# Seven block products instead of eight in the first feed-forward matmul too

## The chip, the cores and the metric

One NeuronCore of one Trainium2 chip. The metric is the device time of one launch in microseconds (us), taken as the median of several runs; one further execution was recorded by the hardware profiler, and all rows below are of that execution.

## The reference

One decoder layer over 512 tokens of width 1024, all in float32: a mixer (a gated chunk MLP beside a state-space scan), a feed-forward layer and a gated per-layer embedding, with a final RMSNorm. The part that the change touches is

```python
hid = jax.nn.relu(rmsnorm(h, norm_mlp_g[i]) @ w_ff1[i])   # (512 x 1024) @ (1024 x 4096)
h = h + (hid * hid) @ w_ff2[i]                            # (512 x 4096) @ (4096 x 1024)
gate = jax.nn.sigmoid(rmsnorm(h, ple_norm_g[i]) @ w_ple_gate[i])
h = h + gate * (p[i] @ w_ple_proj[i])
```

## The kernel before

Every large product is computed from operands split in two: `hi` is the value rounded to float32r, `lo` is what is left. A product of two split operands takes three matmuls, hi by hi, hi by lo and lo by hi (`product`, L1485 to L1489). ScalarE writes a `hi` (a copy with rounding), VectorE then the `lo` (value minus `hi`). An operand tile has 128 partitions; one matmul uses a 128x128 stationary block and streams up to 512 columns into a PSUM bank. There are eight banks: `acc` has four and `side` has four.

The stages in order: the input projection with the mixers beside it (L1567 to L1662), the output projection, the PLE product (L1695 on), whose result ScalarE brings to `y` and SyncE stores to `ple_dram`, the feed-forward layer, the gate product and the output.

The feed-forward layer goes in four units `u` of 1024 hidden columns. Inside a unit there are forms: weight blocks of 512x512, each kept as hi and lo in a ring of three (`ring`). The first matrix gives four forms (`product_f1`, L1705): the whole normed x (in `b_hi`, `b_lo`, transposed, 512 tokens) streams against them, two forms add up in one PSUM bank, four banks per half unit; that is 4 forms x 4 blocks x 4 k-tiles x 3 matmuls of 512 columns. ScalarE applies relu and square bank by bank (`relu`, `square`, L668 to L685).

The second matrix is done in the Strassen-Winograd way: the hidden block (512 tokens x 1024) and the weight block (1024 x 1024) are cut in quarters, and seven products of a sum of quarters with a sum of quarters replace the eight of the plain way (`product_f2`, L1724; PRODUCTS and A_FORMS, L22 and L23). The sums of hidden quarters, S1 to S4, are made by VectorE (`s_add`, L1296). The sums of weight quarters, T1 to T4, are made by GpSimd's queue: DMAs that add one SBUF tile to another (`t_add`, L549), or, for T1, that add a quarter from HBM to a reloaded one (`reload_b12`, L440). Four buffers `quarter` hold the quarters. A form of the second matrix has 2 x 4 x 3 = 24 matmuls of 512 columns. Two of its seven products stay in `side` over all units; the other five go to `acc` and VectorE adds them to `h` (`h_add`, `h_finish`, L1337 to L1365).

Each engine's order is written out by hand: SyncE's loads from L448 on, ScalarE's list from L892 on, VectorE's from L1367 on, TensorE's from L1748 on. Engines meet in semaphores: `form_hi` and `form_lo` count split half-forms, `ff_step` products, `hid_hi` and `hid_lo` split hidden blocks, `h_added` results. A form is split in two halves of 128x1024 by ScalarE and VectorE (`split_form`, L650 and L1286) once the product three forms back has ended. After the last unit the transposes `turn_norm(2, ..)` of h (L1552) stand in the middle of the last product and of the gate products, and `split_gate` (L591 and L995) prepares the gate's weights.

Of the kernel before, what the change touches and what calls it, by code (L numbers as in the profile page):

```python
# [5 lines left out]
P = 128  # L6
F32 = mybir.dt.float32
# [11 lines left out]
TILES = (2, 3, 0, 1)  # L19
UNITS = 4  # L20
STEPS = 30
# [4 lines left out]
SUMS = ("T3", "T2", "T1", "T4")  # L26


def build_layer(nc, a, out):
# [26 lines left out]
    with ExitStack() as ctx:  # L56
# [8 lines left out]
        with ExitStack() as early:  # L65
# [6 lines left out]
            gain = sb("gain", [P, 2, D], where=early)  # L72

        def form(name, tiles, width):

            hi = sb(name + "_hi", [P, tiles, width], F32R)
            with ExitStack() as first:
                raw = sb(name + "_raw", [P, tiles, width], where=first)
            lo = sb(name + "_lo", [P, tiles, width], F32R)
            return hi, raw, lo  # L80

        quarter = [sb(f"quarter{i}", [P, 4, 512]) for i in range(2)]
        ring = {0: form("ring0", 4, 512)}
        ring[2] = form("ring2", 4, 512)
        ring[1] = form("ring1", 4, 512)
        quarter += [sb(f"quarter{i}", [P, 4, 512]) for i in range(2, 4)]
        a2 = form("a2", 4, 512)
        s_form = {n: form(f"s{n}", 4, 256) for n in (3, 4, 1, 2)}
        a1 = sb("a1", [P, 4, 512])
        tmp = sb("tmp", [P, 4, 512])  # L90
        with ExitStack() as early:
            conv = sb("conv", [P, 2, 512], where=early)
            xs_t = sb("xs_t", [P, 2, 512], where=early)
# [3 lines left out]
        a11_hi = sb("a11_hi", [P, 4, 256], F32R)  # L97
        a11_lo = sb("a11_lo", [P, 4, 256], F32R)
# [17 lines left out]
        b_hi = sb("b_hi", [P, KT, SEQ], F32R)  # L116
        b_lo = sb("b_lo", [P, KT, SEQ], F32R)
# [77 lines left out]
        f1_landed = [[sem(f"f1_landed{i}{p}") for p in range(2)] for i in range(3)]  # L195
        q_landed = [[sem(f"q_landed{i}{p}") for p in range(2)] for i in range(4)]
        ff_step = sem("ff_step")
        form_hi, form_lo = sem("form_hi"), sem("form_lo")
        gate_hi, gate_lo = sem("gate_hi"), sem("gate_lo")
        t_landed = [[sem(f"t_landed{i}{p}") for p in range(2)] for i in range(2)]  # L200
# [72 lines left out]
        plan += [(("xt", 2, j, q), (2 * j + q + 2) % 4) for j in range(NS) for q in range(2)]  # L273
# [25 lines left out]
        def form_end(n):  # L299

            u, j = divmod(n, FORMS)
            return STEPS * u + (4 * j + 4 if j < 4 else 16 + 2 * (j - 4) + 2)

        def f1_use(n):

            return sum(m % 3 == n % 3 and m % FORMS < 4 for m in range(n + 1))

        def product_end(u, name):

            return STEPS * u + 16 + 2 * PRODUCTS.index(name) + 2  # L310

        def form_count(u, name, p):

            return 2 * (FORMS * u + 4 + PRODUCTS.index(name)) + p + 1

        def hid_bank(u, i):

            return (i + (2 if u else 0)) % 4

        def sum_landed(eng, u, name, p):  # L320

            eng.wait_ge(t_landed[QUARTER[name]][p], 16 * (2 * u + (1 if name in ("T3", "T2") else 2)))

        ADDS = ("T3 right", "T3 above", "T2", "T4", "B21", "B22")
        LAST_ADDS = ("B11 above", "B11 right", "T1 right", "T1 left", "C21", "C12")
# [5 lines left out]
        LO_COUNT = {"A11": 1, "S3": 2, "S2": 3, "S1": 4, "A22": 6, "A12": 6, "S4": 7}  # L331
# [5 lines left out]
        def _(sp):  # L337
# [71 lines left out]
            def load_f1(n):  # L409

                u, e = divmod(n, FORMS)
                b, kh = 2 * u + e // 2, e % 2
                if n >= 3:
                    sp.wait_ge(ff_step, form_end(n - 3))
                else:
                    sp.wait_ge(acc_full, 4 * (OUT + 4) if n < 2 else 4 * (PLE + 1))
# [1396 lines left out]
```

## Time and profile before

| what | value |
|---|---|
| median of 3 runs | 748.6 us (747.29 to 748.61) |
| the profiled execution, its own time | 747.09 us |
| its span, first to last instruction | 745.3 us |
| TensorE busy | 735.0 us, 99% |
| VectorE busy | 454.1 us, 61% |
| ScalarE busy | 382.9 us, 51% |
| GpSimd busy | 107.3 us, 14% |

In the rows PE is TensorE's matmuls, PEld its weight loads, which overlap them, DVE VectorE, ACT ScalarE, POOL GpSimd and SP SyncE. A group of instructions is told by its line in the kernel and by the tiles that it writes and reads. A matmul's duration is its latency; successive matmuls overlap, so their pace is read from their starts. A `[1.38 <-DVE h L1022]` behind a row is idle time of the engine ahead of it and what ended it.

### The profile page before, as it was taken

To read this page: it belongs to the slowest core of one execution; us is meant where nothing else is said; L and a number is where in the kernel's file an instruction comes from. 1 tells how busy PE (TensorE), PEld (TensorE's weight loads), DVE (VectorE), ACT (ScalarE), POOL (GpSimd) and SP (SyncE) were. 2 spreads that over 40 slices of the span, in tenths; PEclk is the share of its full clock that TensorE was granted. 3 is DMA by queue.
4 is the path that set the end of the run, shared out by engine and by line. 5 is a ranking of instruction groups with operands and counts; after the bars stand their busy time and mean duration, and the time that the engine had idled before them with its cause. 6 is when DMAs were issued, how large, how long until landed. Compare 5 with 4: busy or idle time off the path is not lost.

```text
span 745.3 us, 8676 instructions
## 1 busy us (share of the span) xinstructions
PE 735.0 (99%) x3396; PEld 606.4 (81%) x3396; DVE 454.1 (61%) x500; ACT 382.9 (51%) x516; POOL 107.3 (14%) x88
## 2 busy tenths in 40 slices
PE   8999999999999999999999999999999999999996
PEld 7888877788878888888888888888888888888884
DVE  5556794576667465546444952576454942589764
ACT  6524456644674833304564633572266524575775
POOL 1031000766455000000012000020001000200000
PEclk9999999999999999999999999999999999999998
DMA  9732223342241163100976685477727792585311
GB/s 332 210 86 86 87 85 99 124 143 86 93 162 57 57 214 125 58 29 14 373 234 148 140 297 150 84 143 231 227 63 156 192 275 97 118 192 178 106 57 56
DMA packets 47872, 105.58 MB, mean 142 GB/s; under 512 B 4668, under 2 KB 6360, under 8 KB 47832
## 3 DMA queue, kind: packets, MB, share of 16 engines
q1 hardware_dynamic: 40968, 84.03, 33.7%
q0 software_dynamic: 5632, 16.78, 12.4%
q10 hardware_dynamic: 1232, 4.23, 1.6%
q8 instruction: 27, 0.44, 0.2%
q14 instruction: 13, 0.11, 0.0%
HBM read 88.21 MB, written 4.23 MB: 124 GB/s over the span
## 4 chain that ended last, share of the span: by engine, by line
PE 98%; DMA 1%; ACT 0%; issue 0%; DVE 0%; SPq 0%; DVEq 0%
PE acc L1487 28%; PE acc L1489 28%; PE acc L1488 28%; PE side L1549 3%; PE side L1488 2%; PE side L1489 2%; PE side L1487 2%; PE side L1646 2%; PE side L1613 1%; PE side L1653 1%; PE side L1641 1%; DMA gain<-in_norm_mix_g 1%; PE acc L1570 0%; PE side L1593 0%; PE side L1594 0%; PE side L1633 0%
## 5 line engine op out<-in xcount | busy, mean ns | idle before, releaser
L1487 PE MATMUL acc<-w_hi,a_hi 128*128 128x512 f32 x256 | 104.5, 408 | 0.0
L1489 PE MATMUL acc<-w_hi,a_lo 128*128 128x512 f32 x256 | 100.2, 391 | 0.0
L1488 PE MATMUL acc<-w_lo,a_hi 128*128 128x512 f32 x256 | 99.9, 390 | 0.0
L1487 PE MATMUL acc<-b_hi,ring_hi 128*128 128x512 f32 x256 | 99.7, 390 | 0.0
L1489 PE MATMUL acc<-b_hi,ring_lo 128*128 128x512 f32 x256 | 99.7, 389 | 0.0
L1488 PE MATMUL acc<-b_lo,ring_hi 128*128 128x512 f32 x256 | 99.7, 389 | 0.0
L664 ACT ACTIVATE ring_hi<-quarter 128x1024 fp32r<-128x1024 f32 x56 | 56.5, 1051 | 51.3 <-PE acc L1489 34.7
L1293 DVE TENSOR_TENSOR ring_lo<-ring_raw,ring_hi 128x1024 fp32r<-128x1024 f32 x32 | 38.6, 1223 | 67.0 <-ACT ring_hi L664 67.0
L1293 DVE TENSOR_TENSOR ring_lo<-quarter,ring_hi 128x1024 fp32r<-128x1024 f32 x56 | 66.0, 1220 | 17.0 <-ACT ring_hi L664 17.0
L568 POOL DMA_DIRECT2D quarter<-quarter x24 | 20.8, 868 | 351.1 <-DMA quarter<-in_w_ff 223.1
L993 DVE TENSOR_TENSOR w_lo<-w_raw,w_hi 128x1024 fp32r<-128x1024 f32 (+1 forms) x40 | 50.8, 1272 | 27.9 <-ACT w_hi L587 27.4
L664 ACT ACTIVATE ring_hi<-ring_raw 128x1024 fp32r<-128x1024 f32 x32 | 33.8, 1056 | 59.3 <-DMA ring_raw<-in_w_ff 59.3
L1487 PEld LDWEIGHTS acc<-w_hi,a_hi 128*128 128x128 f32 x256 | 48.2, 188 | 11.1 <-issue 1.4
L1488 PEld LDWEIGHTS acc<-w_lo,a_hi 128*128 128x128 f32 x256 | 48.2, 188 | 10.6 <-issue 1.4
L1489 PEld LDWEIGHTS acc<-w_hi,a_lo 128*128 128x128 f32 x256 | 48.1, 188 | 10.4
L1488 PEld LDWEIGHTS acc<-b_lo,ring_hi 128*128 128x128 f32 x256 | 48.1, 188 | 10.0
L1487 PEld LDWEIGHTS acc<-b_hi,ring_hi 128*128 128x128 f32 x256 | 48.1, 188 | 10.0
L1489 PEld LDWEIGHTS acc<-b_hi,ring_lo 128*128 128x128 f32 x256 | 48.1, 188 | 9.9
L1487 PE MATMUL acc<-w_hi,b_hi 128*128 128x512 f32 x128 | 50.5, 395 | 0.0
L1489 PE MATMUL acc<-w_hi,b_lo 128*128 128x512 f32 x128 | 50.0, 391 | 0.0
L1488 PE MATMUL acc<-w_lo,b_hi 128*128 128x512 f32 x128 | 49.9, 390 | 0.0
L587 ACT ACTIVATE w_hi<-w_raw 128x1024 fp32r<-128x1024 f32 (+1 forms) x40 | 40.2, 1007 | 15.9 <-PE acc L1489 13.7
(231 smaller groups left out, 1471.8 us busy)
## 6 DMA issues: line engine op xcount, KB each, us to landing
quarter<-in_w_ff SPq DMA_DIRECT2D x40, 512.0 KB, 4.8
w_raw<-in_w_in SPq DMA_DIRECT2D x36, 512.0 KB, 3.7
ring_raw<-in_w_ff SPq DMA_DIRECT2D x32, 512.0 KB, 4.9
quarter<-quarter POOLq DMA_DIRECT2D x24, 512.0 KB, 6.1
w_raw<-in_w_out SPq DMA_DIRECT2D x16, 512.0 KB, 3.4
h<-in_x SPq DMA_DIRECT2D x8, 512.0 KB, 4.3
seg<-cs_dram ACTq DMA_DIRECT2D x8, 512.0 KB, 3.9
quarter<-in_w_ff POOLq DMA_DIRECT2D x8, 512.0 KB, 6.3
```

The costliest lines, as they stand in the source:

```text
L568: pool.dma_start(quarter[QUARTER[name]][at], src, accum_op=ALU.add).then_inc(t_landed[QUARTER[name]][p], 16)
L587: act.activation(w_hi[:, half, 2 * p:2 * p + n, :], w_raw[:, p, 0:n, :], ACT.Copy, scale=scale).then_inc(hi_ready, 1)
L664: act.activation(hi[at], src, ACT.Copy).then_inc(form_hi, 1)
L993: ins = dve.tensor_tensor(lo, raw, hi, ALU.subtract)
L1293: dve.tensor_tensor(lo[at], src, hi[at].bitcast(F32), ALU.subtract).then_inc(form_lo, 1)
L1487: pe.matmul(dst, st[0], mv[0], start=start, stop=False)
L1488: pe.matmul(dst, st[0], mv[1], start=False, stop=False)
L1489: return pe.matmul(dst, st[1], mv[0], start=False, stop=stop)
L1549: ins = pe.transpose(bank[:, i * P:i * P + P], src(i), ident[:])
L1613: filled(pe.matmul(bank.rearrange("p (c n) -> p c n", c=NS), wsT[:, g, :], h[:, :, g * P:g * P + P], start=True, stop=True), ("mix", g))
L1641: filled(pe.matmul(bank, bcT[:, 2 + g, at], carry[:], start=True, stop=True), ("off", j))
L1646: ins = pe.matmul(bank[:, r * HD:r * HD + HD], lm[:, r, :], xdt[:, r * HD:r * HD + HD], start=True, stop=True)
```

## The change

The first feed-forward matrix is now done in the same way as the second: per unit seven products of 512x512 weight forms with 512x256 blocks of x. The blocks of x (A11, A12, A22 and S1 to S4, each hi and lo) are made once, ahead of unit 0 and in it, and kept. A unit has 14 forms (FORMS), seven of each matrix, and all come out of the four `quarter` buffers; the ring's raw buffers are gone. A product of the first matrix writes four half banks (`pair`), 4 x 4 x 3 matmuls of 256 columns. ScalarE copies two products (P1, P3) from PSUM, VectorE combines all seven into the four hidden quarters (`combine`), and relu and square work on whole quarters. For both matrices T3, T2 and T4 are made by GpSimd's accumulating DMAs, and T1 by VectorE, as T2 minus B22, in place of the DMA from HBM (`make_t1`). The order of the second matrix's products changes, results go to other banks, the PLE result gets a buffer of its own, and the tiles of the gate go in the order 0 to 3. The diff, cut to its core:

```diff
-TILES = (2, 3, 0, 1)
+TILES = (0, 1, 2, 3)
-FORMS = 11
-PRODUCTS = ("B11", "T3", "T2", "T1", "T4", "B21", "B22")
-A_FORMS = ("A11", "S3", "S2", "S1", "A22", "A12", "S4")
-QUARTER = {"T3": 0, "T1": 0, "B12": 0, "B11": 1, "T2": 1, "T4": 1, "B21": 2, "B22": 3}
+FORMS = 14
+FIRST = ("B11", "B21", "B22", "T2", "T3", "T1", "T4")
+FIRST_A = ("A11", "A12", "S4", "S2", "S3", "S1", "A22")
+SECOND = ("B11", "B21", "T3", "T2", "B22", "T1", "T4")
+SECOND_A = ("A11", "A12", "S3", "S2", "S4", "S1", "A22")
+QUARTER = {"T3": 0, "B12": 0, "B11": 1, "T2": 1, "B21": 2, "T4": 2, "B22": 3}
+def home(m, name):
+    return (3, 0)[m] if name == "T1" else QUARTER[name]
...
 SyncE, per unit:
-                load_quarter(u, "B12")
-                load_quarter(u, "B11")
-                load_quarter(u, "B21")
-                load_f1(FORMS * u)
-                load_quarter(u, "B22")
-                for e in range(1, 4):
-                    load_f1(FORMS * u + e)
-                reload_b12(u)
+                load_quarter(u, 1, "B12")
+                load_quarter(u, 1, "B11")
+                load_quarter(u, 1, "B22")
+                load_quarter(u, 1, "B21")
+                if u < UNITS - 1:
+                    load_quarter(u + 1, 0, "B11")
+                    load_quarter(u + 1, 0, "B22")
+                    load_quarter(u + 1, 0, "B12")
+                    load_quarter(u + 1, 0, "B21")
...
 ScalarE, per unit:
+                both(2)
+                copy_product(u, "P1")
+                if u == 0:
+                    x_split("S2")
+                both(3)
+                if u == 0:
+                    x_split("S3")
+                both(4)
+                hidden(u, "A11")
+                copy_product(u, "P3")
+                if u == 0:
+                    x_split("S1")
+                    x_split("A22")
+                split_a(u, "A11")
+                both(5)
+                both(6)
+                both(7)
+                both(8)
+                hidden(u, "A12")
+                split_a(u, "A12")
+                hidden(u, "A22")
+                both(9)
+                hidden(u, "A21")
+                split_a(u, "S3")
+                both(10)
+                split_a(u, "S2")
+                split_a(u, "S4")
+                both(11)
+                both(12)
+                split_a(u, "S1")
+                both(13)
+                split_a(u, "A22")
+                if u < UNITS - 1:
+                    both(14)
+                    both(15)
...
 VectorE:
+            def make_t1(u, m, p):
+                at = (slice(None), slice(2 * p, 2 * p + 2))
+                sum_landed(dve, u, m, "T2", p)
+                dve.wait_ge(form_lo, form_count(u, m, "T3" if m else "B22", p))
+                dve.tensor_tensor(quarter[home(m, "T1")][at], quarter[1][at], quarter[3][at], ALU.subtract
+                                  ).then_inc(t1_made, 1)
+            def combine(u, what):
+                dst, left, right, op = {
+                    "C11": ("A11", "A21", pair(1), ALU.add), "U": ("A21", pair(1), "A21", ALU.subtract),
+                    "C12 part": ("A12", "A12", "A21", ALU.add), "U3": ("A21", "A21", pair(0), ALU.add),
+                    "C12": ("A12", "A12", pair(1), ALU.add), "C22": ("A22", "A21", pair(1), ALU.add),
+                    "C21": ("A21", pair(0), "A21", ALU.subtract)}[what]
...
 VectorE, per unit, both(j) is two split_form:
+                if u:
+                    h_add(u - 1, "T4")
+                both(2)
+                both(3)
+                combine(u, "C11")
+                for p in range(2):
+                    make_t1(u, 0, p)
+                both(4)
+                both(5)
+                split_a(u, "A11")
+                combine(u, "U")
+                combine(u, "C12 part")
+                both(6)
+                combine(u, "U3")
+                both(7)
+                combine(u, "C12")
+                combine(u, "C22")
+                both(8)
+                combine(u, "C21")
+                split_a(u, "A12")
+                both(9)
+                s_add(u, "S3")
+                s_add(u, "S1")
+                split_a(u, "S3")
+                both(10)
+                s_add(u, "S2")
+                s_add(u, "S4")
+                h_add(u, "B21")
+                split_a(u, "S2")
+                for p in range(2):
+                    make_t1(u, 1, p)
+                both(11)
+                h_add(u, "T3 right")
+                h_add(u, "T3 above")
+                split_a(u, "S4")
+                both(12)
+                h_add(u, "T2")
+                split_a(u, "S1")
+                both(13)
+                split_a(u, "A22")
+                if last:
+                    h_finish("B11 above")
+                    h_finish("B11 right")
+                h_add(u, "B22")
+                if not last:
+                    both(14)
+                    both(15)
...
+            split_gate(0, 0)
+            h_finish("T1 right")
+            h_finish("C12")
+            split_gate(0, 1)
...
 TensorE:
+            def product_f1(u, j):
+                if j < 2:
+                    pe.wait_ge(*((h_added, add_count(u - 1, ("B22", "T4")[j])) if u else emptied(PLE, 2 + j)))
+                elif j in (2, 4):
+                    pe.wait_ge(p_copied, 2 * u + j // 2)
+                else:
+                    pe.wait_ge(combined, combined_count(u, {3: "C11", 5: "U", 6: "U3"}[j]))
                 for i in range(4):
                     for k in range(4):
                         if i == 0 and k % 2 == 0:
                             pe.wait_ge(form_lo, 2 * n + k // 2 + 1)
+                        ins = product(pair(j % 2)[:, i, :], [t[:, k, i * P:i * P + P] for t in (hi, lo)],
+                                      [t[name][:, k, :] for t in (x_hi, x_lo)], k == 0, k == 3)
...
+                if name == "B21":
+                    pe.wait_ge(combined, combined_count(u, "C22"))
+                elif name == "T3":
+                    pe.wait_ge(combined, combined_count(u, "C21"))
+                elif not kept:
+                    pe.wait_ge(h_added, add_count(u, {"T2": "B21", "B22": "T3 above", "T4": "T2"}[name]))
...
 TensorE, turn_norm of the tail:
-                    pe.wait_ge(h_last, len(LAST_ADDS))
-                    pe.wait_ge(h_added, add_count(UNITS - 1, "B22" if s else "T4"))
+                    pe.wait_ge(h_last, LAST_ADDS.index("T1 left" if s else "C12") + 1)
+                    pe.wait_ge(h_added, add_count(UNITS - 1, "T4" if s >= 2 else "B22"))
```

## Rows read from the trace of the kernel before

**Rows 1.** The page: busy times, the chain by engine; the waits of TensorE.

```profile
PE 735.0 (99%) x3396; PEld 606.4 (81%) x3396; DVE 454.1 (61%) x500; ACT 382.9 (51%) x516; POOL 107.3 (14%) x88
...
PE 98%; DMA 1%; ACT 0%; issue 0%; DVE 0%; SPq 0%; DVEq 0%
...
PE acc L1567 <- POOL ident L496: 1.7, 1, 1.7
PE side L1549 <- DVE h L1022: 1.4, 1, 1.4
```

**Rows 2.** Groups by line and form: busy us, mean ns; feed-forward and PLE matmuls.

```profile
L1487 PE MATMUL acc<-b_hi,ring_hi 128*128 128x512 f32 x256 | 99.7, 390 | 0.0
...
L1487 PE MATMUL acc<-ring_hi,s_hi 128*128 128x512 f32 x88 | 34.3, 390 | 0.0
...
L1487 PE MATMUL acc<-ring_hi,a_hi 128*128 128x512 f32 x64 | 24.9, 390 | 0.0
...
L1487 PE MATMUL side<-ring_hi,s_hi 128*128 128x512 f32 x40 | 15.7, 392 | 0.0
...
L1487 PE MATMUL side<-ring_hi,a_hi 128*128 128x512 f32 x32 | 12.5, 390 | 0.0
...
L1487 PE MATMUL acc<-w_hi,p_hi 128*128 128x512 f32 x16 | 6.4, 402 | 0.0
```

**Rows 3.** Timeline, first matrix: start, length in us, engine, line, tiles.

```profile
380.07 0.39 PE L1487 MATMUL acc<-b_hi,ring_hi 128*128 128x512 f32 x1
...
382.79 0.39 PE L1487 MATMUL acc<-b_hi,ring_hi 128*128 128x512 f32 x1
```

**Rows 4.** Busy us of each engine in one unit, granted clock, DMA share, GB/s.

```profile
core 0: us, PE busy (x) PEld busy (x) DVE busy (x) ACT busy (x) POOL busy (x), PEclk, DMA share, GB/s
443.20:524.80 81.60, 81.60 (x362) 67.60 (x361) 45.90 (x43) 38.36 (x45) 7.47 (x8) 1.00 0.63 167
```

**Rows 5.** Weight loads, ns min/median/max: of float32r matmuls, then of fp32 ones.

```profile
L1487 PEld LDWEIGHTS acc<-b_hi,ring_hi x256: 187/188/188, 364.2 to 651.8; 128*128 128x128 f32 x128
...
L1633 PEld LDWEIGHTS side<-bcT x16: 188/188/193, 140.5 to 240.9; 128*128 128x128 f32 x16
```

**Rows 6.** Timeline of TensorE at the start.

```profile
7.74 1.09 PE L1549 MATMUL side<-ident,h 128*128 128x128 f32 x8 [1.38 <-DVE h L1022]
8.67 2.40 PE L1570 MATMUL acc<-ones,ident 128*128 128x128 f32 x20
10.82 0.48 PE L1487 MATMUL acc<-w_hi,a_hi 128*128 128x512 f32 x1
```

**Rows 7.** Timeline of VectorE in unit 1; its groups of h adds and gate splits.

```profile
495.52 2.35 DVE L1332 TENSOR_TENSOR s_lo<-s_raw,s_hi 128x1024 fp32r<-128x1024 f32 x2
...
502.33 2.54 DVE L1350 TENSOR_TENSOR h<-h,acc 128x1024 f32<-128x1024 f32 x2
...
L1350 DVE TENSOR_TENSOR h<-h,acc 128x1024 f32<-128x1024 f32 x23 | 28.0, 1219 | 24.8 <-PE acc L1489 24.3
...
L1000 DVE SCALAR_TENSOR_TENSOR w_lo<-w_raw,cols,w_hi 128x512 fp32r<-128x512 f32 x16 | 11.0, 749 | 1.5 <-ACT w_hi L596 1.5
```

**Rows 8.** Timeline of ScalarE in unit 1: relu, square, splits.

```profile
459.83 0.60 ACT L674 ACTIVATE tmp<-acc 128x512 f32<-128x512 f32 x1 [4.63 <-PE acc L1489]
460.46 0.63 ACT L685 ACTIVATE a<-tmp 128x512 f32<-128x512 f32 x1
...
494.71 2.00 ACT L695 ACTIVATE a_hi<-a_raw 128x1024 fp32r<-128x1024 f32 x2
```

**Rows 9.** Timeline of TensorE in the last product.

```profile
687.88 0.39 PE L1489 MATMUL side<-ring_hi,s_lo 128*128 128x512 f32 x1
688.11 1.03 PE L1549 MATMUL side<-ident,h 128*128 128x128 f32 x8
```

**Rows 10.** DMA issues: each half MB, median us to landing.

```profile
quarter<-in_w_ff SPq DMA_DIRECT2D x40, 512.0 KB, 4.8
...
quarter<-quarter POOLq DMA_DIRECT2D x24, 512.0 KB, 6.1
```

More of the change, by code:

```diff
@@ L72, in build_layer @@
             gain = sb("gain", [P, 2, D], where=early)
[L74 to L91, printed above, removed]
+            tmp = sb("tmp", [P, 4, 512], where=early)
             conv = sb("conv", [P, 2, 512], where=early)
             xs_t = sb("xs_t", [P, 2, 512], where=early)
+        def split_pair(name, tiles, width):
+            return sb(name + "_hi", [P, tiles, width], F32R), sb(name + "_lo", [P, tiles, width], F32R)
@@ new lines, in raw_lo, with raw_hi @@
+        def raw_lo(name):
+            with ExitStack() as first:
+                raw = sb(name + "_raw", [P, 4, 256], where=first)
+            return raw, sb(name + "_lo", [P, 4, 256], F32R)
+        def raw_hi(name):
+            with ExitStack() as first:
+                raw = sb(name + "_raw", [P, 4, 256], where=first)
+            return raw, sb(name + "_hi", [P, 4, 256], F32R)
+        quarter = [sb(f"quarter{i}", [P, 4, 512]) for i in range(2)]
+        ring = {0: split_pair("ring0", 4, 512)}
@@ new lines, in build_layer @@
+        ring[2] = split_pair("ring2", 4, 512)
+        ring[1] = split_pair("ring1", 4, 512)
+        quarter += [sb(f"quarter{i}", [P, 4, 512]) for i in range(2, 4)]
+        with ExitStack() as early:
+            g_hi = sb("g_hi", [P, KT, SEQ], F32R, where=early)
+            g_lo = sb("g_lo", [P, KT, SEQ], F32R, where=early)
+        x_hi, x_lo, x_raw = {}, {}, {}
+        for name in ("A11", "A12"):
+            x_hi[name], x_lo[name] = split_pair("x" + name, 4, 256)
+        x_raw["A11"], x_hi["S2"] = raw_hi("xA11_S2")
@@ L297, in freed, with form_of @@
             ins.then_inc(side_free[fills[name][0]], 1)
-        def form_end(n):
+        def form_of(n):
             u, j = divmod(n, FORMS)
[L302 to L325, printed above, removed]
+            return u, j // 7, (FIRST + SECOND)[j]
+        def form_index(u, m, name):
+            return FORMS * u + 7 * m + (FIRST, SECOND)[m].index(name)
@@ L327, in add_count, with combined_count @@
+        ADDS = ("B21", "T3 right", "T3 above", "T2", "B22", "T4")
+        LAST_ADDS = ("B11 above", "B11 right", "T1 right", "C12", "T1 left", "C21")
         def add_count(u, what):
             return 2 + len(ADDS) * u + ADDS.index(what) + 1
-        LO_COUNT = {"A11": 1, "S3": 2, "S2": 3, "S1": 4, "A22": 6, "A12": 6, "S4": 7}
+        COMBINED = ("C11", "U", "C12 part", "U3", "C12", "C22", "C21")
+        def combined_count(u, what):
+            return 7 * u + COMBINED.index(what) + 1
+        HID = ("A11", "A12", "A22", "A21")
@@ L687, in split_a @@
[L687 to L698 removed]
+                i = home(m, name)
```

630 lines of the change are left out of this document (313 added, 317 removed).

## The prediction

> **What bounds the kernel now.** First the page: the tensor engine is busy 99% of the span and is 98% of the chain that ended last [rows 1]. Then its waits: two, 3.1 us together, both in the first 8 us [rows 1]. So the time is the number of TensorE columns times their pace, and the other engines only have to keep up. Then the groups by line: in the feed-forward part the first product is 3 x 256 = 768 matmuls of 512 columns, the second 3 x (88 + 64 + 40 + 32) = 672 [rows 2]; over four units that is 192 and 168 each. The listed 389 ns is a matmul's latency; its pace must be read from starts: twelve from 380.07 to 382.79, 226.7 ns each [rows 3]. 360 x 226.7 ns = 81.6 us, the width of one unit's window, in which VectorE is busy 45.9 us, ScalarE 38.4 us, the DMA engines 63% [rows 4].
>
> **TensorE's side.** The new first product is seven block products of 4 x 4 x 3 = 48 matmuls of 256 columns, so 336 half-width matmuls in place of 192 full ones: columns equal to 168, an eighth less. At exactly half price (113.3 ns) a unit's first product goes from 43.5 to 38.1 us, 5.4 us less; TensorE alone breaks even at 43.5/336 = 129.5 ns. No float32r matmul of 256 columns is in the trace. 512 columns at 2.4 GHz are 213.3 ns, so the row has 13.3 ns more per matmul, and the question is whether that halves. Also every matmul has its own weight load: 188 ns of latency, the same as for plain fp32 loads [rows 5]. What it occupies is seen where streams are short: twenty fp32 matmuls that stream 107 ns each, one load apiece, fill 8.67 to 10.9 us, about 111.5 ns each [rows 6]. So the floor is 111.5 ns (the load), the upper end the load plus the surplus, 111.5 + 13.3 = 125 ns. I take 106.7 + 13.3 = 120.0 ns: the surplus per instruction unchanged, because the nearest row is the same instruction at twice the width, and nothing in it says that what is left over per instruction depends on the width. First product: 336 x 120.0 = 40.3 us, 3.2 us less per unit, 12.8 us in all (21.8 at half price, 24 at the floor, 6.4 at 125 ns). The second product keeps its 168 matmuls.
>
> The Trainium skill ("TensorE: Matmul & The Clock Gate", Back-to-back issue gap) gives a gap of N/2.4 plus 2.5 ns, 109 ns at 256 columns; at 512 it says 216 where the row has 227, so the trace does not agree for this operand type. The same page (LDWEIGHTS) puts a load at columns/1.2, 107 ns, which the 111.5 ns pace supports, and which speaks against narrow matmuls.
>
> **VectorE's side: the new stall.** Per unit VectorE now splits 14 forms instead of 11 (two instructions each), makes T1 (4), combines the seven products (7), forms four sums, splits seven A blocks and adds six results: 28+4+7+4+7+6 = 56 of 128x1024. Before it had 43 instructions in a unit, six of them half width [rows 4]. ScalarE gets six more half-form splits and two copies of products, and its sixteen half-width relu and square instructions become eight of full width; it stays under 50 us of 78. Paces: independent instructions start 1.135 us apart (two in 2.35, busy 1.22), one that waits for its predecessor's result 1.32 (two in 2.54 us) [rows 7]; PSUM sources cost the same. ScalarE: 0.95 us apart (two in 2.00, busy 1.05); where square waits for relu it starts 0.03 after its end, so 1.08 [rows 8]. 56 x 1.15 = 64 us of 78 (40.3 + 38.1): it fits on average, so the order decides.
>
> Take the two queues in the order of the diff, and count from the end of the first matrix's last product (T4), t = 0. C21 needs it: VectorE 0.05. A12's low part 1.2. ScalarE meanwhile, held by C12 and C22 (the product T1 ended at -5.8), does two splits, relu, square, A12's split, relu, square and reaches form 9 at 1.3, relu and square of A21 at 3.2 and 4.3, done 5.4. VectorE: form 9 at 2.4 and 3.5; S3 only at 5.4, S1 6.5, S3's low part 7.7 (after ScalarE's high part), form 10 at 8.9 and 10.0, S2 11.1, S4 12.5 (it waits for S2), B21 into h 13.6, S2's low part 14.7, T1 at 15.9 and 17.0, form 11 at 18.1 and 19.3, T3 into h 20.4 and 21.7 (dependent), S4's low part 22.9 to 24.1. TensorE wants, at 5.44 us a product: T3 at 10.7 (S3 ready 9.0), T2 at 16.2 (S2 ready 16.0, just), B22 at 21.6, whose A block is S4: ready 24.1, and restarting takes a semaphore and one weight load, some 0.3 us. **Stall 2.8 us a unit.** Without any idle time or dependence those 20 instructions would end near 23.4, so 2.0 is its least; 3.5 if releases cost more. After it VectorE is ahead again: S1 ready 28.6 for 29.8, form 13 and A22 32.0 for 35.2, B22 into h 33.2, the next unit's forms 35.5 and 38.8 for 40.8 and 46.2.
>
> In the first matrix I find the same walk free: C11, two T1 instructions and form 4 end 5 to 6 us before their product, U 4 us, U3 4 us. TensorE waits for copies P1 and P3 have a whole product (5.8 us) for one 1.05 us copy. Unit 0 has in addition five x splits, four x sums and the two h adds: form 7 to C22 slip, C21 starts 2.9 us late, S3 2.0: **2.0 us more, once**.
>
> Tail: the transposes that stand inside the last product now wait for C12, behind B11 twice, B22, two gate splits (0.66 us apart, busy 0.75) and T1. My walk: T1 product done 35.4, T1 right 36.9, C12 38.2 to 39.4, transposes 39.7 where TensorE is there at 38.0: **1.7 us**. The transposes now stand in the chain without a wait [rows 9]. T1 left and T4 come before the transposes that need them.
>
> DMA: a unit now takes sixteen half-quarter loads of 512 KB from SP (it took eighteen) and twelve accumulating ones from POOL (it took eight), 6.1 us each against 4.8 for a load [rows 10]. I cost this at nothing; what hides it is slack. The tightest chain crosses the unit: B12 is reloaded after form 12 (t = 26.4), lands 31.5, T3 38, T2 44.5; ScalarE wants T2 at 47.5, TensorE at 58. Three us of cover, then ten more before TensorE notices. The PLE stores stay behind four quarter loads as before. The edits ahead of unit 0 (x kept as blocks, raw copies by ScalarE in place of VectorE's splits, the PLE result in a buffer of its own) lie under PLE's matmuls, 3 x 16 of them [rows 2], 10.9 us; without that cover two copies and two splits would be late, some 4 us. The new order of the tiles costs nothing.
>
> **Sum.** -12.8 + 4 x 2.8 + 2.0 + 1.7 = +2.1 us. The profiled execution took 747.1 us (span 745.3), the median of three runs is 748.6, 1.5 above it; I carry that: 748.6 + 2.1 = **750.7 us**. With the stall between 2.0 and 3.5 this case alone spans 747.5 to 753.5.
>
> **Rivals.**
> B, the surplus halves with the width or vanishes under the load (111.5 to 115 ns): for it, the load's own pace; against it, nothing but the argument above. Savings 21.8, stalls 3.1 x 4 (ScalarE reaches form 9 later relative to TensorE) + 2.8 + 1.7 = 16.9: -4.9, **743.7 us**; at the floor and the least stall about 738. The skill's gap formula, named above, points to this rival.
> C, the other side: load and stream hinder each other, 125 ns. Saving 6.3 less 14.9: +8.6, **757 us**. This side begins at 118.4 ns, where 4 x 336 matmuls save just the 14.9 us of the stalls (174.1 - 14.9 = 159.2 us). A pause at each B22 could also cost the clock: the granted clock is 1.00 throughout [rows 4], and after the only idle stretch of comparable kind, 1.38 us at 7.74, the transposes ran at the 2.4 GHz pace (eight in 1.09 us) [rows 6]; if it did fall to 1.2 GHz for some us after each stall, the price is 1 to 3 us a unit, the same side.
> D, late transfers: T2 of the first matrix more than 10 us late, from a DMA share already at 63% [rows 4]: 2 to 4 us in three units, about 760.
> E, the narrow matmul is not a single pass: 213 ns and more, 336 x 0.213 = 72 us, +110 us, 860. No row speaks for it; then the change does not do what it says.
>
> **Chances.** Forecast 0.42, B 0.38, C 0.12, D 0.05, E 0.03. 0.2% is about what a measurement of this kernel can tell (1.5 us). Faster is nearly all of B and the low edge of the forecast, 0.41; within 0.2%: 0.16; slower 0.43. Range 739 to 759: it leaves out E, D's upper part and B's last edge. The forecast's own range is 747.5 to 753.5.
>
> **What would show it.** Pace of the 256-column matmuls: 120 (113 for B, 125 for C). TensorE idle ahead of B22 of the second matrix, 2.8 us, released by VectorE's low part of S4, four times; 2 us more in unit 0; 1.7 us at the last transposes. VectorE with 56 instructions in a unit and hardly any idle time in the 18 us before the stall. No idle in a first product. Unit windows 81.2 us against 81.6. It is wrong if the stall sits elsewhere, if TensorE waits for ring_hi of a T form (D), or if the pace is over 130 ns.

## The result, and the profile after

Four runs of the changed kernel took 758.27 to 766.67 us, median **765.3 us**, beside 747.9 us for the kernel before on the same chip (747.23 to 748.61): a ratio of 1.021 (95% interval 1.015 to 1.028). The forecast was 750.7 us, the range 739 to 759. The sign is that of the larger chance, but only just (slower 0.43, faster 0.41), and the size is not as forecast: the profiled execution took 764.29 us with a span of 762.55, 17.2 us more than before, where the sum had +2.1. The changed kernel also scatters by 8 us where the one before keeps to 1.4.

The page of the changed kernel, against [rows 1]: busy times, the granted clock in 40 slices, the chain by engine.

```profile
PE 734.2 (96%) x3972; PEld 629.6 (83%) x3972; DVE 538.5 (71%) x561; ACT 416.7 (55%) x525; POOL 118.2 (16%) x104
...
PEclk9999999999999999999999899999999999999898
...
PE 67%; DVE 16%; ACT 8%; DMA 5%; issue 4%; DVEq 0%; SPq 0%; ACTq 0%
```

TensorE was 98% of the chain before; now a third of it runs through other engines, VectorE first. The waits of TensorE say where:

```profile
PE acc L1632 <- DVE fS_lo L1465: 12.7, 6, 2.6
PE acc L1632 <- DVE w_lo L1095: 2.9, 1, 2.9
...
PE side L1697 <- DVE h L1495: 1.4, 1, 1.4
PE acc L1632 <- DVE fA_lo L1465: 0.8, 1, 0.8
```

And the stretches: what lies ahead of the feed-forward part, the four units (columns as in [rows 4]), the gate and output.

```profile
0.00:367.20 367.20, 363.89 (x1732) 299.45 (x1733) 227.90 (x265) 189.11 (x261) 79.55 (x59) 1.00 0.39 124
367.20:455.40 88.20, 82.54 (x506) 73.90 (x506) 75.93 (x66) 51.68 (x52) 11.14 (x13) 0.96 0.75 189
455.40:536.90 81.50, 79.12 (x506) 71.73 (x505) 65.00 (x56) 45.06 (x45) 9.46 (x11) 1.00 0.72 178
536.90:619.10 82.20, 79.06 (x506) 71.68 (x505) 65.00 (x56) 45.08 (x45) 10.32 (x12) 1.00 0.72 180
619.10:703.00 83.90, 80.06 (x513) 72.42 (x512) 69.95 (x64) 46.55 (x51) 7.74 (x9) 1.00 0.65 176
703.00:762.50 59.50, 49.49 (x217) 40.41 (x216) 34.72 (x56) 39.19 (x72) 0.00 (x0) 0.91 0.16 58
```

A unit took 81.6 us before [rows 4], the last one 82.5. Unit 0 now takes 88.2; no unit reaches the 78.4 us that 40.3 and 38.1 would give.

**The saving is as forecast.** The first matmul of unit 1's first product, the one twelve later, and the first of the second product:

```profile
455.39 0.28 PE L1632 MATMUL acc<-xA_hi,ring_hi 128*128 128x256 f32 x1
...
456.82 0.28 PE L1632 MATMUL acc<-xA_hi,ring_hi 128*128 128x256 f32 x1
...
495.70 0.40 PE L1632 MATMUL side<-ring_hi,fA_S_hi 128*128 128x512 f32 x1
```

336 matmuls in 40.31 us are 120.0 ns each, in all four units, with no pause between them: 4 x (43.52 - 40.31) = 12.8 us saved.

**The forecast stall is there too.** VectorE ahead of B22 in unit 1, then TensorE's restart:

```profile
507.43 1.22 DVE L1458 TENSOR_TENSOR fS_raw<-fA_S_raw,fS_raw 128x1024 f32<-128x1024 f32 x1
508.69 1.23 DVE L1458 TENSOR_TENSOR fS_raw<-fA_raw,fS_raw 128x1024 f32<-128x1024 f32 x1
509.83 1.21 DVE L1482 TENSOR_TENSOR h<-h,acc 128x1024 f32<-128x1024 f32 x1
510.96 1.22 DVE L1465 TENSOR_TENSOR fS_lo<-fS_raw,fA_S_hi 128x1024 fp32r<-128x1024 f32 x1
512.10 2.35 DVE L1424 TENSOR_TENSOR quarter<-quarter 128x1024 f32<-128x1024 f32 x2
514.37 2.35 DVE L1417 TENSOR_TENSOR ring_lo<-quarter,ring_hi 128x1024 fp32r<-128x1024 f32 x2
516.64 2.54 DVE L1482 TENSOR_TENSOR h<-h,acc 128x1024 f32<-128x1024 f32 x2
519.09 1.22 DVE L1465 TENSOR_TENSOR fS_lo<-fS_raw,fA_S_hi 128x1024 fp32r<-128x1024 f32 x1
...
520.37 0.50 PE L1632 MATMUL acc<-ring_hi,fA_S_hi 128*128 128x512 f32 x1 [2.36 <-DVE fS_lo L1465]
```

No idle time between any two of these. From start to start beyond its pace, TensorE loses 2.43, 2.52, 2.52 and 2.55 us at this place in the four units.

**Three things were not in the sum.** First, the reload of B21. In unit 0 ScalarE waits for both its halves, for form 8:

```profile
396.29 2.01 ACT L757 ACTIVATE ring_hi<-quarter 128x1024 fp32r<-128x1024 f32 x2 [3.75 <-PE acc L1634]
404.69 1.06 ACT L757 ACTIVATE ring_hi<-quarter 128x1024 fp32r<-128x1024 f32 x1 [6.39 <-DMA quarter<-in_w_ff]
408.50 1.06 ACT L757 ACTIVATE ring_hi<-quarter 128x1024 fp32r<-128x1024 f32 x1 [2.75 <-DMA quarter<-in_w_ff]
```

SyncE may issue that reload only once form 6 (T4 of the first matrix, in the same buffer) has its low part; VectorE wrote it from 396.6 to 398.9, and the two halves landed at 404.67 and 408.48, 6.9 and 9.5 us after their issue. Relu and square of A12, A22 and A21 stand behind form 8 on ScalarE, and S3 behind them: pauses of 0.99 us before B21, 2.73 before T3 and then 2.43 before B22. The same reload is late in the other units too, by less. In unit 2 ScalarE waits 0.96 us for it and TensorE then loses 0.95 us ahead of T2 (0.20 and 0.18 in unit 1, 0.15 and 0.14 in unit 3):

```profile
573.69 1.06 ACT L757 ACTIVATE ring_hi<-quarter 128x1024 fp32r<-128x1024 f32 x1 [0.96 <-DMA quarter<-in_w_ff]
...
594.47 0.50 PE L1632 MATMUL acc<-ring_hi,fA_S_hi 128*128 128x512 f32 x1 [0.79 <-DVE fS_lo L1465]
```

Second, behind two of these pauses and behind a later one the matmuls ran at the 1.2 GHz level, 427 ns apart instead of 227: 7 of them from 424.0, 6 from 438.0, 12 from 722.0, together 5.0 us. Third, the gate:

```profile
705.66 1.22 DVE L1495 TENSOR_TENSOR h<-h 128x1024 f32<-128x1024 f32 x1
...
708.24 1.21 DVE L1482 TENSOR_TENSOR h<-h,acc 128x1024 f32<-128x1024 f32 x1
...
709.48 1.06 ACT L688 ACTIVATE tmp<-h 128x1024 f32<-128x1024 f32 x1 [1.99 <-DVE h L1482]
...
712.24 2.55 ACT L664 ACTIVATE w_hi<-w_raw,cols 128x512 fp32r<-128x512 f32 x4
...
719.96 2.74 DVE L1095 SCALAR_TENSOR_TENSOR w_lo<-w_raw,cols,w_hi 128x512 fp32r<-128x512 f32 x4 [1.00 <-ACT w_hi L664]
...
721.43 0.79 PE L1632 MATMUL acc<-w_hi,g_hi 128*128 128x512 f32 x1 [2.86 <-DVE w_lo L1095]
```

T4 is added to h at 708.2, five us after its product ended, behind T1, C21 and gate splits; ScalarE's sums of squares wait for that, and the second half of the gate's weights stands behind the sums: ScalarE starts on its first part at 712.24 and, behind the output of the first tile, on its last part at 719.23. TensorE waits for that last part. From the last feed-forward matmul to the end of the span it is 59.7 us against 53.9 before.

Against the 745.3 us of before: -12.8 (first product); +21.3 in the second products (9.8, 3.1, 3.8, 4.7 in the four units); +5.9 behind the feed-forward part; +2.8 ahead of it. Sum 17.2. The last 2.8 us are in the first 14 us of the kernel, where nothing changed:

```profile
9.71 4.46 PE L1718 MATMUL acc<-ones,ident 128*128 128x128 f32 x20
13.83 0.56 PE L1632 MATMUL acc<-w_hi,a_hi 128*128 128x512 f32 x1
```

The twenty matmuls took 2.40 us and the first wide one began at 10.82 before [rows 6]; here most of them are 213 ns apart. The seven variants of the changed kernel below have the same start, and in their profiles that first one begins anywhere from 10.93 to 12.60 us. The granted clock shows why in one of them (the variant `a_gate`), where it stood at half from 8.5 to 11.8 us:

```profile
8.50:11.80 3.30, 3.30 (x17) 3.30 (x16) 2.83 (x4) 3.30 (x5) 0.00 (x0) 0.50 1.04 407
```

So the start varies by execution, and most or all of these 2.8 us belong to it. In the four profiles of the kernel before and its variants that matmul begins at 10.82 to 10.99; that no share of the 2.8 us comes with the change is not shown.

### The profile page after: what moved, and what is told of

Read it like the earlier page. It is cut to its first block, busy times and chain, and to the rows that moved or that the text cites. A ratio compares the mean times of both kernels' runs of the same rounds, so it can differ in the third digit from the quotient of the medians.

```text
span 762.5 us, 10007 instructions
## 1 busy us (share of the span) xinstructions
PE 734.2 (96%) x3972; PEld 629.6 (83%) x3972; DVE 538.5 (71%) x561; ACT 416.7 (55%) x525; POOL 118.2 (16%) x104
## 3 DMA queue, kind: packets, MB, share of 16 engines
q0 software_dynamic: 6912, 25.17, 17.7%
## 4 chain that ended last, share of the span: by engine, by line
PE 67%; DVE 16%; ACT 8%; DMA 5%; issue 4%; DVEq 0%; SPq 0%; ACTq 0%
PE acc L1632 19%; PE acc L1634 19%; PE acc L1633 19%; DVE ring_lo L1417 5%; DMA quarter<-in_w_ff 4%; PE side L1697 3%; ACT ring_hi L757 2%; DVE fS_lo L1465 2%; DVE fS_raw L1458 2%; PE side L1794 2%; DVE h L1482 2%; ACT fA_S_hi L790 1%; DVE quarter L1424 1%; ACT fA_raw L769 1%; PE side L1761 1%
## 5 line engine op out<-in xcount | busy, mean ns | idle before, releaser
L757 ACT ACTIVATE ring_hi<-quarter 128x1024 fp32r<-128x1024 f32 x112 | 113.6, 1051 | 98.2 <-PE acc L1634 73.2
L1417 DVE TENSOR_TENSOR ring_lo<-quarter,ring_hi 128x1024 fp32r<-128x1024 f32 x112 | 132.5, 1221 | 39.3 <-ACT ring_hi L757 39.3
L1633 PE MATMUL acc<-xS_lo,ring_hi 128*128 128x256 f32 x256 | 72.4, 283 | 0.0
L1088 DVE TENSOR_TENSOR w_lo<-w_raw,w_hi 128x1024 fp32r<-128x1024 f32 x36 | 48.1, 1337 | 27.9 <-ACT w_hi L656 27.5
L1634 PE MATMUL acc<-xA_hi,ring_lo 128*128 128x256 f32 x192 | 54.3, 283 | 0.0
L1632 PE MATMUL acc<-xS_hi,ring_hi 128*128 128x256 f32 x192 | 54.3, 283 | 0.0
L1634 PE MATMUL acc<-xS_hi,ring_lo 128*128 128x256 f32 x192 | 54.3, 283 | 0.0
L1633 PE MATMUL acc<-xA_lo,ring_hi 128*128 128x256 f32 x192 | 54.3, 283 | 0.0
L1632 PE MATMUL acc<-xA_hi,ring_hi 128*128 128x256 f32 x192 | 54.3, 283 | 0.0
L1633 PEld LDWEIGHTS acc<-xS_lo,ring_hi 128*128 128x128 f32 x256 | 49.2, 192 | 0.0
L656 ACT ACTIVATE w_hi<-w_raw 128x1024 fp32r<-128x1024 f32 (+1 forms) x40 | 40.1, 1006 | 16.2 <-PE acc L1634 13.7
```

Source lines behind the costliest of these rows:

```text
L656: act.activation(w_hi[:, half, at, :], w_raw[:, p, 0:n, :], ACT.Copy, scale=scale).then_inc(hi_ready, 1)
L757: act.activation(ring[n % 3][0][at], quarter[i][at], ACT.Copy).then_inc(form_hi, 1)
L1088: ins = dve.tensor_tensor(lo, raw, hi, ALU.subtract)
L1417: dve.tensor_tensor(lo[at], src, hi[at].bitcast(F32), ALU.subtract).then_inc(form_lo, 1)
L1632: pe.matmul(dst, st[0], mv[0], start=start, stop=False)
L1633: pe.matmul(dst, st[0], mv[1], start=False, stop=False)
```

## The experiments

**One stall at a time.** Four variants of the changed kernel. The first moves the second half of the gate's weights ahead of the last sums, on both engines (ScalarE's list; VectorE's in the same way ahead of `root(2)` and `root(3)`).

```diff
             xt_evac(2, 1)
+            split_gate(1, 0)
+            split_gate(1, 1)
             sums(2, 2)
             sums(2, 3)
+            split_gate(1, 2)
+            split_gate(1, 3)
...
-                if i < 2:
-                    for p in (2 * i, 2 * i + 1):
-                        split_gate(1, p)
```

> The changed kernel with one move at the end: ScalarE and VectorE split the gate weights' second half before the last two square sums and roots, where they stood behind them. Theory (waits and clock): in the profile of the changed kernel TensorE stands still for about 3.1 us ahead of the third gate product, and the 13 matmuls behind it run at 427 ns instead of 227, 2.7 us more; both go, so the time falls by 5 to 6 us and the time from the last feed-forward matmul to the last matmul returns from 52.2 us to about 46.3. Rival (the time at the end is lost to VectorE's load, whatever its order): the pause appears at another gate product and the time stays within 1 us.

758.4 us (757.33 to 760.16). From the last feed-forward matmul to the end it is 53.8 us, as before the change, and the wait for `w_lo` is gone. So the path from the sums to the splits explains all 5.9 us there. The order itself was the same in the kernel before, but there the second half's splits began 6.0 us behind the last feed-forward matmul, in the changed kernel 9.4. The edit leaves the feed-forward part alone: the wait for `fS_lo` stands at 13.0 us. In this profile that part is 1.9 us longer, with 27 matmuls 427 ns apart instead of 13.

The second makes the second matrix's T1 behind S4's low part instead of ahead of form 11.

```diff
                 split_a(u, "S2")
-                for p in range(2):
-                    make_t1(u, 1, p)
                 both(11)
                 h_add(u, "T3 right")
                 h_add(u, "T3 above")
                 split_a(u, "S4")
+                for p in range(2):
+                    make_t1(u, 1, p)
```

> The changed kernel with one move in VectorE's list: the two subtractions that make T1 of the second matrix come after S4's low part instead of before form 11. Theory (VectorE's order): the pause ahead of the second matrix's B22 falls from about 2.5 us to 0.3 in each unit, a pause of up to 0.6 us appears ahead of the T1 product; 6 to 8 us less over four units, and some 1.6 us more where unit 0's third pause had lowered the clock. Rival (VectorE is simply too busy): the pause moves to the T1 product at full size, and the time stays within 1 us.

756.6 us (755.05 to 757.43). The pause before B22 fell to 0.29 us in units 1 to 3, and no matmul in units 1 and 2 ran at 1.2 GHz. But TensorE now waits before the product with T1, which I had put at 0.6 us at most:

```profile
PE side L1632 <- DVE fS_lo L1465: 4.5, 4, 1.1
PE acc L1632 <- DVE fS_lo L1465: 3.4, 2, 2.2
```

The first row is the product with T1 (1.28 us from start to start in each unit), the second is in unit 0. Half of what was removed came back one product later. Units 1 and 2 take 80.3 us. The last unit is 1.4 us longer than in the changed kernel: the pause at the last transposes grew from 1.61 to 2.51 us, and the clock fell behind it.

The third splits form 6 right behind form 5, ahead of four other VectorE instructions.

```diff
                 both(5)
+                both(6)
+                combine(u, "U")
                 if u == 0:
                     x_split("A22")
-                split_a(u, "A11")
-                combine(u, "U")
                 combine(u, "C12 part")
-                both(6)
+                split_a(u, "A11")
```

> The changed kernel with one move in VectorE's list: form 6 of the first matrix is split right after form 5, before U, C12's part and A11. Theory (late reload): SyncE issues the load of B21 for the second matrix once form 6 is split, in unit 0 at 397.8 and 399.0 us, and it lands at 404.7 and 408.5, where ScalarE would take it near 399; issued about 3.5 us earlier, unit 0 loses its first pause (1.0 us) and much of the second (2.7 us), and with them the slow stretch behind it (1.6 us): 3 to 5 us less, all in unit 0, units 1 to 3 unchanged within 0.5 us. Rival (unit 0 is late because VectorE has five x splits and two h adds more there): unit 0 keeps its pauses within 1 us.

756.1 us (754.51 to 756.35). ScalarE at form 8, and TensorE's waits:

```profile
400.52 2.01 ACT L757 ACTIVATE ring_hi<-quarter 128x1024 fp32r<-128x1024 f32 x2 [3.75 <-PE acc L1634]
...
PE acc L1632 <- DVE fS_lo L1465: 10.7, 5, 2.4
```

The reload is issued at 391.6 and 392.7, lands at 399.2 and 400.6, and form 8 waits for nothing but its place in the ring. Unit 0 takes 82.8 us instead of 88.2: the chain form 6, reload of B21, form 8 was worth up to 5.4 us there. Both falls of the clock are in that number, and one of them, 1.2 us behind B22, stayed away although its pause did not (2.56 us): that share is luck. In units 1 to 3 no pause ahead of T2 is left. The landing still took 7.6 and 7.9 us. So what made form 8 late is when the transfer began; its length is only part of it.

The fourth left the waits alone and filled unit 0's with matmuls whose result nothing uses (eleven of 512 columns before T3, four before B22).

> The changed kernel with extra matmuls in unit 0 that are overwritten later: eleven of 512 columns in the wait ahead of the second matrix's T3 product, four ahead of its B22 product, each in a stretch in which TensorE stands still. No wait of another engine changes. Theory (idle time lowers the clock): the two stretches of unit 0 in which matmuls take 427 ns, eight or nine each, go or shrink, the time falls by 1.5 to 3.5 us, and the waits for S3 and S4 keep their ends. Rival (the clock falls for another reason, load or heat): the 427 ns stretches stay and the time stays within 1 us or grows.

765.9 us (763.75 to 767.47), no gain. In its profile unit 0 has no stretch at 1.2 GHz and takes 85.9 us instead of 88.2. But units 1 to 3 take 84.9, 85.3 and 86.8: form 8 waits 2.0 to 2.8 us for its reload there, pauses of 0.5 to 1.4 us stand ahead of T3 and T2, and the clock fell behind the pause at B22 in each. Why the reload is later in these units was not looked into, so this run neither shows nor rules out that filling a pause keeps the clock up; as a remedy it gave no gain.

**All three together.**

> The changed kernel with three earlier edits together: the second half of the gate weights split ahead of the last sums and roots; the second matrix's T1 made behind S4's low part; form 6 split right behind form 5. Theory (three separate stalls, each with its own late instruction): the single gains of 6.9, 8.7 and 9.2 us add, -24.8 us against the changed kernel, 740 to 743 us, about 1% under the kernel before. Left over: a pause of about 1.3 us before the product with T1 of the second matrix in every unit, and 2.5 us at the last transposes. Rival (VectorE simply has too much to do, so that a stall removed in one place comes back at the next): less than half of the sum, 752 us or more.

747.6 us (746.04 to 747.98), ratio 0.999 (0.998 to 1.000) to the kernel before. That is 17.7 us gained, not 24.8, and neither theory: two of the three edits had each claimed the same stretches of unit 0 and the same falls of the clock (3.8 and 5.4 us of unit 0 alone, 6.2 together). The single gains also held 1.4 to 2.6 us of an earlier start in the profiles, which is no effect of an edit, and the reference median of 765.3 comes from four runs that scatter by 8 us. In the profiles, the four units and the gate are 9.5 and 5.9 us shorter, and no feed-forward matmul is at 1.2 GHz.

> As the three edits together, and T2 added into h only behind form 12 and S1's low part, and the first gate split behind C12 in the tail. Theory: the 1.3 us pause before T1's product goes in units 1 to 3, and the last transposes come about 1 us earlier: 4 to 5 us less than the three edits alone, 735 to 738 us; units of 79 us or less. Rival: TensorE waits next for T2's add into h (the bank of the product T4) or for form 12, and the gain is under 1.5 us.

VectorE's list against the three edits together (the move of the gate split is left out):

```diff
                 both(12)
-                h_add(u, "T2")
                 split_a(u, "S1")
+                both(12)
+                h_add(u, "T2")
```

749.2 us (748.79 to 750.75), 1.6 us slower than the three edits alone. The pause before T1's product stayed at 1.2 us, now released by form 12's low part, and VectorE had 2 us of idle time ahead of S1's low part. ScalarE shows why:

```profile
510.08 2.20 ACT L757 ACTIVATE ring_hi<-quarter 128x1024 fp32r<-128x1024 f32 x2 [6.31 <-DVE quarter L1425]
512.18 1.04 ACT L790 ACTIVATE fA_S_hi<-fS_raw 128x1024 fp32r<-128x1024 f32 x1
```

S1's high part stood behind form 12, which waits for T1 to be made, though VectorE had made S1 by 494.9. In the last unit the wait at the transposes grew to 3.35 us, with a fall of the clock behind it. The next kernel takes that order out, on ScalarE, and shortens what is ahead of S4.

```diff
-                both(12)                  # ScalarE
                 split_a(u, "S1")
+                both(12)
...
-                both(11)                  # VectorE
+                split_form(n + 11, 0)
                 h_add(u, "T3 right")
                 h_add(u, "T3 above")
                 split_a(u, "S4")
+                split_form(n + 11, 1)
```

> As a_all2, and ScalarE rounds S1 before form 12 instead of behind it, and VectorE splits the second half of form 11 only behind S4's low part. Theory (in a_all2 the pause before T1's product was inherited from ScalarE: S1's high part stood behind form 12, which had waited 6.3 us for T1 to be made): the pause of 1.2 us goes in all four units and the 0.27 us before B22 too, so a unit takes 78.7 us and the kernel 742 to 744 us, 0.6 to 0.8% under the kernel before. The pause at the last transposes stays at 2.5 to 3.4 us. Rival (VectorE's total is the bound behind T3): VectorE without idle time over the whole stretch, and a pause of 1 us or more somewhere between B22 and T4.

**741.0 us** (739.49 to 743.51), ratio 0.990 (0.989 to 0.992) to the kernel before: 1% faster than it, and 24 us faster than the change as it was made. Its four units:

```profile
365.90:445.90 80.00, 78.79 (x505) 71.67 (x504) 73.47 (x65) 50.81 (x52) 9.44 (x11) 1.00 0.73 194
445.90:524.40 78.50, 78.50 (x506) 71.82 (x505) 64.81 (x57) 44.94 (x46) 10.35 (x12) 1.00 0.74 187
524.40:602.80 78.40, 78.40 (x505) 71.77 (x504) 64.79 (x57) 44.94 (x45) 10.34 (x12) 1.00 0.73 188
602.80:688.10 85.30, 82.39 (x513) 74.82 (x513) 73.78 (x68) 49.57 (x56) 8.62 (x10) 0.96 0.71 187
...
PE side L1700 <- DVE h L1496: 2.9, 1, 2.9
...
PE acc L1635 <- DVE fS_lo L1466: 1.2, 1, 1.2
```

Units 1 and 2 are busy from end to end at 78.4 and 78.5 us, with the same work on VectorE (64.8 us busy, 65.0 in the changed kernel). VectorE's total was never the bound; the order was, on two engines. ScalarE's edit and VectorE's were made together, so what each is worth alone is not shown. What is left in this profile, the slowest of the six runs, is 3.1 us at the last transposes (C12) with 2.8 us behind it, in which transposes and matmuls ran at the 1.2 GHz level, and 1.4 us in unit 0.

**The pace by width**, in the kernel before. Each unit's first products are cut at other columns (`cuts`), and each half of their sum over the rows is written alone, so the result leaves the first half out.

```diff
+                    cuts = ((0, 256, 512), (0, 128, 256, 384, 512), (0, 384, 512), (0, 320, 512))[u]
+                    for c, d in zip(cuts, cuts[1:]):
...
+                            ins = product(acc[:, hid_bank(u, i), c:d], [t[:, k, i * P:i * P + P] for t in (hi, lo)],
+                                          [t[:, 4 * kh + k, c:d] for t in B], k == 0, k == 3)
```

> The kernel before, with its first products cut into narrower matmuls, another width in each unit: 2 x 256 columns in unit 0, 4 x 128 in unit 1, 384 and 128 in unit 2, 320 and 192 in unit 3; each half of the sum over the rows is written alone, so that the first half of it is left out of the result. Theory (a fixed surplus per matmul over its columns at 2.4 GHz, 13.3 ns, at any width until the weight load of about 111 ns takes over): 256 columns 120.0 ns, 320 columns 146.7, 384 columns 173.3, 192 and 128 columns at the load's floor of 107 to 115 ns. Rival (256 columns are paced by the weight load plus something, and the 120 ns are no surplus of the stream): 320 and 384 columns stand on another line than 226.7 and 120.0 ns do, and 192 columns take 120 ns too.

The kernel took 809.5 us. The stretches of the four units' first products:

```profile
364.50:410.60 46.10, 46.10 (x386) 46.08 (x385) 19.24 (x18) 20.16 (x26) 6.00 (x6) 1.00 0.76 221
448.70:534.40 85.70, 85.70 (x769) 85.70 (x768) 18.51 (x17) 19.11 (x25) 4.12 (x4) 1.00 0.30 72
572.60:627.50 54.90, 54.90 (x386) 54.90 (x384) 18.51 (x17) 19.66 (x26) 4.13 (x4) 1.00 0.47 112
665.65:715.10 49.45, 49.45 (x385) 49.45 (x384) 18.51 (x17) 20.16 (x26) 4.12 (x4) 1.00 0.50 116
```

384 matmuls of 256 columns in 46.1 us are 120.0 ns; 768 of 128 columns in 85.7 us are 111.6 ns, the load's floor of [rows 6]. Most starts of 384-column matmuls are 173 or 174 ns apart, of 320-column ones 146 or 147, of 192-column ones 110 to 112. So the time is the columns at 2.4 GHz plus 13.3 ns at each of the four widths from 256 to 512, and at 192 and 128 columns the floor. The rival is out. The Trainium skill ("TensorE: Matmul & The Clock Gate", Back-to-back issue gap) has 2.5 ns in place of the 13.3; no width here agrees with that for this operand type.

**Pauses and the clock**, in the kernel before. TensorE waits at chosen places for a chain of small VectorE instructions on a buffer of their own; `JUNK` sets how many.

```diff
+            def hold(i, step):
+                dve.wait_ge(ff_step, step)
+                for c in range(JUNK[i - 1] if i else 0, JUNK[i]):
...
+                        dve.tensor_scalar(junk[:], junk[:], 1.0, None, ALU.mult).then_inc(junk_done, 1)
```

> The kernel before with twelve forced pauses of TensorE, three a unit, each behind a chain of two to five small VectorE instructions on data that nothing uses: about 1.3, 1.8, 2.3 and 2.8 us, three times each, in mixed order. Its matmuls are all 512 wide. Theory (a pause alone brings the granted clock down for the matmuls behind it, if it is long enough): no fall behind the pauses under 2 us, a fall to 1.2 GHz behind most of those from 2.3 us on, each 1.0 to 1.6 us dear; the sum of pauses 25 us and of falls 4 to 8 us. Rival (the changed kernel's falls come from its 256-column matmuls, or from the number of its weight loads, not from the pauses): no fall behind any pause here.

807.1 us. VectorE was still at other work at two of the three places, so the pauses came out longer: 0.87, 1.20, 1.53, 1.86 us, then eight of 3.39 to 6.90. Behind the four short ones the clock stayed up, behind each of the eight 6 to 12 matmuls ran 427 ns apart. All matmuls here are 512 wide, so the pause alone does it, and the narrow ones are not to blame.

> The kernel before with one forced pause of TensorE in each unit, at the start of the second product, where VectorE was on time: 6, 7, 8 and 9 small VectorE instructions of 0.33 us, so pauses of 2.2, 2.5, 2.8 and 3.2 us. Up to here pauses up to 1.86 us left the clock alone and pauses from 3.4 us on brought it down every time. Theory: in between the fall is a matter of where the pause lies against something periodic, so the four pauses show falls at some and not at others, and surely at 3.2. Rival (a fixed length decides): all above one of the four lengths, none under it.

761.5 us, pauses of 2.25, 2.51, 2.84 and 3.17 us. The three us behind each:

```profile
410.30:413.30 3.00, 3.00 (x13) 2.50 (x14) 2.63 (x5) 1.09 (x2) 0.00 (x0) 1.00 0.59 108
494.55:497.55 3.00, 3.00 (x7) 2.42 (x8) 2.69 (x5) 0.84 (x1) 0.00 (x0) 0.50 0.42 76
580.69:583.69 3.00, 3.00 (x13) 2.49 (x14) 2.69 (x5) 0.50 (x1) 0.00 (x0) 1.00 0.37 68
665.61:668.61 3.00, 3.00 (x7) 2.42 (x8) 2.69 (x5) 0.17 (x1) 0.00 (x0) 0.51 0.36 66
```

7 matmuls instead of 13, clock 0.5, behind the pause of 2.51 us, and none lost behind the longer one of 2.84: the length alone does not decide, and the rival is out. Over the profiles of all these kernels (pauses from 360 us on, read from starts):

| pause before it | how many | clock fell behind it |
|---|---|---|
| 0.87 to 2.25 us | 34 | 0 |
| 2.39 to 2.91 us | 26 | 17 |
| 3.07 to 6.90 us | 11 | 11 |

The stall of 2.5 us lies in the middle row. That fits the scatter of the changed kernel, whose mean clock in the four runs was 0.984 to 0.992; what decides between fall and no fall in that row was not tried.

## Why the prediction was wrong

Two paths that the prediction put at nothing failed, and with them a term that it priced only in a rival: the reload of B21 ("I cost this at nothing; what hides it is slack"), the path from T4's add over the sums of squares to the gate's weights, and the clock's fall behind pauses of 2.4 us and more.

**The pace, right.** "The surplus per instruction unchanged": 120.0 ns measured, 12.8 us saved, in the sum as in the trace. Rivals B and C fall by it, E too. (By its own terms, 24 us saved against 12.5 us of stalls, B's lower end was 737 us and not 738.) The width experiment shows the rule behind it and not only the value. The floor had been read off twenty fp32 matmuls at 111.5 ns whose own streams the prediction puts at 107 ns; that row could not tell load from stream. Float32r matmuls of 128 columns, 53.3 ns at 2.4 GHz, at 111.6 ns do.

**The stall before B22, right.** 2.8 us a unit forecast; 2.43 to 2.55 plus 0.1 us of restart measured, at the instruction named, with VectorE free of idle time ahead of it. The low part of S4 ended 24.4 us behind the first matrix's last product, against 24.1 in the walk; the restart took 0.1 us instead of 0.3.

**The reload of B21, the step that failed first.** For unit 0 the prediction had "2.0 us more, once", with C21 and S3 late behind the x splits and sums. Beyond the stall at B22 there were 3.7 us of pauses, 0.99 and 2.73. The forecast named a tightest chain of the DMAs, from B12's reload to T3 and T2, and costed all transfers at nothing on its slack. That chain held. The one that broke, from form 6 to the reload of B21 to form 8, was never walked. It is late in every unit, by 0.15 to 0.96 us in units 1 to 3, where it shows ahead of T2 ("S2 ready 16.0, just"), and by 6.4 and 2.8 us in unit 0, where VectorE has more to do. Undone alone, it gave back 5.4 us of that unit, 1.2 of them luck with the clock. It is rival D in kind, but D was placed at T2 of the first matrix and in three units.

**The clock, a term left out of the sum.** The text had the fall behind a stall as a side remark in rival C, at "1 to 3 us a unit", from one counterexample of 1.38 us of idle time [rows 6]. The pause forecast was twice as long, and at that length the clock fell in 17 cases of 26, 1.0 to 1.6 us each. By these counts, which no row of before could give, the term is an estimated 4 x 2/3 x 1.3 = 3.5 us. In this execution it was 5.0 us, two falls in unit 0 and one in the gate.

**The tail.** "1.7 us" at the last transposes: 1.61 measured, released by C12, right. "T1 left and T4 come before the transposes that need them" is true, and this is the second step that failed, since the prediction's walk of the tail ends there. What needed T4 was the sum of squares on ScalarE, and behind it, in program order, the splits of the gate's weights. That is 5.9 us, 2.4 of them the clock, and moving the splits alone brought all of it back.

**The account.** Forecast +2.1; the pause at B22 -0.7; more pauses in unit 0 +1.9; small pauses ahead of T2 in the other units +1.6; the clock in unit 0 +2.6; the gate +5.9; the start of this execution +2.8: 16.2 of 17.2. The missing 1.0 us is not placed.

## What to carry to other kernels

Here the two stalls named by a walk through the queues came out within 0.3 us, and a later, shorter walk (the pause ahead of T1's product) missed by 0.7; what had not been walked cost most. When a change loads an engine to 80% and more, walk every buffer's chain from release over reload to first use, and every instruction queued behind a waiting one, up to the end of the kernel and not only to the next matmul. Put the clock's fall into the sum as soon as a pause comes near 2.5 us. And when removing a late instruction only moves the pause to the next product, look at the other engine's order before blaming the load: with 56 VectorE instructions in a unit either way, it went from 81.5 and 82.2 to 78.4 and 78.5 us by order alone.

## What had not been expected

The floor under a float32r matmul with its own weight load is 111.6 ns at 128 columns and 110 to 112 at 192. By an estimate from these two and the 13.3 ns, a narrower matmul is no faster between 128 and some 236 columns (111.6 - 13.3 = 98.3 ns at 2.4 GHz). Quarter loads got longer: 6.9 and 9.5 us for the two late halves in unit 0, a median of 5.8 in the changed kernel, 4.8 before [rows 10]. The changed kernel has twelve accumulating DMAs a unit beside them instead of eight, but no run tells whether these do it. The clock did not fall behind a pause of 2.84 us and fell behind one of 2.43. And the start of the kernel, unchanged, differs by up to 3 us between the profiles, by when the warming matmuls reach the 2.4 GHz pace.
